# Moving four of a quad's 26 gather operations from the output half to the first-projection half of an expert stage on one Trainium2 core

## The reference

```
g = jax.nn.softmax(cv, axis=-1)
a = jax.nn.gelu(jnp.einsum('td,thkd->thk', tb, u_tab[e]).astype(jnp.float32), approximate=False)
return jnp.einsum('thk,thkd->td', (g * a).astype(tb.dtype), v_tab[e])
```

## Time and profile before

| | |
|---|---|
| median of 3 runs | 4360.06 us (4358.92 to 4373.73) |
| the profiled execution's own time | 4361.63 us |
| its span, first to last instruction | 4359.9 us |
| stage of the experts, within the span | about 2350 to 4280 us |
| busy over the span: PE, DVE, ACT, POOL | 80%, 63%, 31%, 38% |
| DMA over the span | 1001.69 MB, mean 230 GB/s |

### The profile page before, as it was taken

How to read it: one execution, slowest core, us unless ns; L and a number is a source line. 1 busy time by engine, 2 the same in 40 slices (tenths; PEclk the granted TensorE clock), 3 DMA queues, 4 the chain that set the end, 5 groups by cost and what they waited for, 6 DMA issues and landing times. The chain is left out here.

```text
span 4359.9 us, 58885 instructions
## 1 busy us (share of the span) xinstructions
PE 3499.7 (80%) x20213; PEld 2842.0 (65%) x20213; DVE 2764.6 (63%) x5857; ACT 1344.7 (31%) x3219; POOL 1641.3 (38%) x1339
## 2 busy tenths in 40 slices
PE   6899967846577668625665999999999999999995
PEld 1344335521144468625555999999999999999994
DVE  0011148610113403899995998888989989999985
ACT  0111136610001111137783333333333333333331
POOL 0000000000000143238885565565556655556650
PEclk9899979977768889867777999999999999999997
DMA  9345144489931133305547988989889888888984
GB/s 348 133 173 179 60 141 151 133 337 408 406 143 35 50 109 98 96 29 117 129 106 226 324 323 310 323 313 323 319 307 329 322 323 314 318 321 324 322 308 161
DMA packets 390819, 1001.69 MB, mean 230 GB/s; under 512 B 186132, under 2 KB 236143, under 8 KB 327832
## 3 DMA queue, kind: packets, MB, share of 16 engines
q1 hardware_dynamic: 324232, 487.39, 32.7%
q0 software_dynamic: 64144, 474.73, 30.1%
q10 hardware_dynamic: 2272, 37.68, 2.4%
HBM read 914.75 MB, written 152.04 MB: 245 GB/s over the span
## 5 line engine op out<-in xcount | busy, mean ns | idle before, releaser
L1904 DVE CUSTOM_DVE_ANT_0 e_uv<-e_uv,e_h 128x1024 f32<-128x1024 f32 x416 | 720.9, 1733 | 73.4 <-DMA e_uv<-peer_uv,k_g_idx 71.4
L1973 POOL DMA_INDIRECT e_uv<-peer_uv,k_g_idx x416 | 519.5, 1249 | 534.7 <-DVE e_pY L1916 493.5
L1212 PE MATMUL e_pa<-k_hi_d,e_uh 128*128 128x320 f32 x2048 | 639.0, 312 | 65.4 <-POOL e_ul L1964 55.8
L1212 PE MATMUL e_po<-e_ph,e_vh 128*128 128x320 f32 x2048 | 645.0, 315 | 54.3 <-DVE k_OT L1948 49.1
L1214 PE MATMUL e_pa<-k_hi_d,e_ul 128*128 128x320 f32 x2048 | 633.7, 309 | 0.0
L1213 PE MATMUL e_pa<-k_lo_d,e_uh 128*128 128x320 f32 x2048 | 633.7, 309 | 0.0
L1214 PE MATMUL e_po<-e_ph,e_vl 128*128 128x320 f32 x2048 | 632.7, 309 | 0.0
L1213 PE MATMUL e_po<-e_pl,e_vh 128*128 128x320 f32 x2048 | 632.6, 309 | 0.0
L1916 DVE SCALAR_TENSOR_TENSOR e_pY<-e_uv,e_wts,e_pY 128x1024 f32<-128x1024 f32 x412 | 526.1, 1277 | 0.0
L1212 PEld LDWEIGHTS e_pa<-k_hi_d,e_uh 128*128 128x128 f32 x2048 | 385.3, 188 | 77.4 <-issue 64.4
L1212 PEld LDWEIGHTS e_po<-e_ph,e_vh 128*128 128x128 f32 x2048 | 384.3, 188 | 76.6 <-DVE k_OT L1948 63.0
(11 more groups left out here) (280 smaller groups left out, 5460.5 us busy)
## 6 DMA issues: line engine op xcount, KB each, us to landing
s_kv<-kv_pages SPq DMA_DIRECT2D x128, 512.0 KB
s_kv<-kv_state SPq DMA_DIRECT2D x32, 2048.0 KB
e_u<-peer_ut SPq DMA_DIRECT2D x128, 512.0 KB, 6.2
e_v<-peer_uv SPq DMA_DIRECT2D x128, 512.0 KB
s_g<-r_G SPq DMA_DIRECT2D x10, 4096.0 KB, 20.8
k_OT<-s_g SPq DMA_DIRECT2D x128, 320.0 KB
k_win_sample<-state_k_win ACTq DMA_DIRECT2D x28, 1168.0 KB
v_win_sample<-state_v_win POOLq DMA_DIRECT2D x28, 1168.0 KB
```

Of the source, the lines that this page charges most:

```text
L1212: nc.tensor.matmul(out, lhs_hi, rhs_hi, start=start, stop=False)
L1904: nc.vector.tensor_tensor_reduce(uv[:, r, 0:D], uv[:, r, 0:D], h[:], 1.0, 0.0, ALU.mult, ALU.add, dots[:, r:r + 1]).then_inc(row_dotted, 1)
L1973: nc.gpsimd.indirect_dma_start(uv[:, s % RING], None, io["peer_uv"], bass.IndirectOffsetOnAxis(ap=keep.g_idx[:, s:s + 1], axis=0),).then_i ...
```

## The change

`share` deals the same 26 operations, in the same order, over the places in another way. Before, every one of the 16 output places has one, and the eight first-half places have 10 between them (1, 1, 1, 2, 1, 1, 1, 2). Now 12 go to the output places (0, 1, 1, 1 in each group of four) and 14 to the first half (1, 2, 2, 2, 1, 2, 2, 2). Nothing else is edited.

```diff
         def share(slot):
 
+            late = OUTS * 3 // 4
             if slot >= DOTS:
-                first = NR - OUTS + slot - DOTS
-                return range(first, first + 1)
-            return range((NR - OUTS) * slot // DOTS, (NR - OUTS) * (slot + 1) // DOTS)
+                n = slot - DOTS
+                return range(NR - late + n * 3 // 4, NR - late + (n + 1) * 3 // 4)
+            return range((NR - late) * slot // DOTS, (NR - late) * (slot + 1) // DOTS)
```

## The result

The changed kernel takes 4408.55 us (median of 4 runs, 4404.33 to 4411.64), the kernel before 4359.81. The ratio is 1.0103, with a 95% interval of 1.0084 to 1.0121: slower by 1.0%, 49 us, little but clear of the noise. The forecast was 4320, and the range ended at 4390. The profiled execution took 4411.64, with a span of 4409.9.

A forecast was written before the change was run, and what follows sets the result against it. VectorE, late all round the 60.1 us quad, was taken as the bound; orders of 59.5 and 57.2 mixed to 58.7, with transfers 58.8, so 1.3 us x 31 = 40 us gained: 4320 us, range 4272 to 4390.

The forecast's parts named there:

- What bounds the kernel: Whole quad of 60.1 us: VectorE is late all round, and TensorE's 3.8 us of standing still follow from it.
- The arithmetic of the path: Quad period: first add at 33.7, plus 0.45, 21.1 of TensorE output work and 4.2 to the next `e_act`, 59.5 us.
- the point of decision: First half: a first add 34.4 us after the first `e_act`, 60.1 - 25.75, beyond which the change is slower.
- Order A: First half with v of block 3 in time, two subtractions without a gap: first add at 33.7, period 59.5 us.
- Rival (2): First half becomes the long pole, with all 2.2 us of transfer wait moved in: period 61.7, 4411 us; chance 0.20.
- I take 0.8 us, nearer to the low end because of the lead: First-half transfer waits per quad, put at 0.8 us because gathers were thought issued 10 us or more before their dots.
- the upper bound of 2.2: First-half transfer waits: at most the kernel before's gather wait of 2.2 us a quad.
- The last sum: Quad period: 58.7 plus half to all of 0.8 for transfers, taken as 58.8, 59.2 at most; gain 40 us.
- The mixture of orders A and B: Quad period over the stage: 0.65 x 59.5 + 0.35 x 57.2 = 58.7 us, before transfer waits.
- B: First half with v of block 3 some tenths late: 2.4 us of block vanish, first add at 31.3, period 57.2 us.
- from there it runs free: TensorE from output place 4, after the first add at 33.7 + 0.45: 21.1 us without holds to the end of the half.
- The bound by the DMA engines: First half's 11.1 MB at about 358 GB/s from HBM for one core: it could not be shorter than 31.0 us.

The follow-up runs named there:

- e9: Changed kernel with the next gather issued ahead of GpSimd's subtraction of v in first-half place 5 only; 4373.27 us, ratio 1.0056.
- e3: Changed kernel with only the first 512 of 1024 columns of u and v loaded for block c + 2; 4409.06 us, ratio 1.0101.
- e7: Changed kernel with GpSimd's subtraction of v done on 512 of 1024 columns from the second quad on; 4311.29 us, ratio 0.9883.
- e1: Changed kernel with the next gather issued ahead of GpSimd's subtraction of v in first-half places 0 and 5; 4481.16 us, ratio 1.026.
- e5: e1 with 8 overwritten TensorE matmuls added ahead of output place 0 of each quad; 4433.97 us, ratio 1.0167.
- e2: Kernel before the change with the next gather issued ahead of GpSimd's subtraction of v in first-half places 0 and 5; 4470.94 us, ratio 1.0248.

## Why the prediction was wrong

**What bounds the kernel: right.** VectorE was late all round; after the change TensorE is busy in the output half, its waits for adds fell from 49.1 to 21.1 us, and VectorE waits for TensorE at the start of a quad. The arithmetic of the path was right in kind, first half + what TensorE then needs, but that term was taken at 25.75 us and came out at 26.4, so that 35.1 makes 61.5 and not 60.9. With 26.4 the point of decision is a first half of 60.1 - 26.4 = 33.7 us, and not 34.4: in e9 33.9 went with a period of 60.3. Order A, laid out at 33.7, stood on this point and had no gain in it. Rival (2), which was given 0.20, had the direction and gave 4411 for what came out as 4408.6; that closeness is luck, since it rests on 59.5 + 2.2 of transfer waits, and 3.5 were measured with half of the blocks.

**The step that failed: "I take 0.8 us, nearer to the low end because of the lead".** The transfer waits of the first half were 3.5 us a quad, over the upper bound of 2.2 too. The ground for it was that "from the issue of a gather to its dot it is 10 us or more in my layout". That was a misreading of my own layout. The gather that follows a sum belongs to the dot five operations later; seven operations later, at place 4, the layout has the 10 us or more. In the layout the gather of place 0 went out at 4.5 (behind the subtraction) and its dot in place 3 could start at 11.8: 7.3 us, and the quad shown has 7.2, of the 9.7 that it needed. The waits of the kernel before come at leads of the same size, 7.4 us in the mean of its output half, so the lead spoke for the upper end of the bound. Packing the operations shortened just this lead; before, this gather went out at 3025.49, its dot came in place 4, and the lead was 10.4 us in the mean.

**The last sum does not follow either.** From the mixture of 58.7, half to all of the 0.8 is 59.1 to 59.5, not 58.8 and "59.2 at most". By its own terms the prediction had a gain of 0.6 to 1.0 us a quad, 19 to 31 us, and not 40.

**The mixture of orders A and B: wrong.** B rested on v of block 3 coming late, in a third of the quads. It was in time in all of them (the trace after has 0.2 us of such waits in total, the one before 15.6). The likely reason is the gather wait in place 3, which puts everything behind it off; the same shift would explain why the blocks, laid out as 8.0, were 4.1, though no run shows either by itself. The errors cancelled: 8.0 of blocks, 0.8 of gather waits and 2.9 for ScalarE on paper, 4.1, 3.5 and 4.1 in the trace, 11.7 both times. About 1.4 of the last stands in place 1, mostly because TensorE is late there. The first half came out at 35.1 instead of 33.7 to 34.5; the 0.6 above the upper end are small gaps, for which the layout had nothing.

**Order A itself was priced too low.** Its first half was near (34.1 in e3), but "from there it runs free" was not right: the hold for `e_pl` of place 6, which comes at 28.3 when TensorE is through with its half at 24.4, was in the layout, and I priced it as nothing but a hold. In most quads of e3 the granted clock falls behind it. The quads of e3 in which this hold stands take 61.6 us with the fall and 60.1 without, not 59.5. So even the case on which the forecast stood was at or above the 60.1 of the kernel before.

**The bound by the DMA engines** was not the cause: e3 with 2.1 MB less a quad took the same time as the change. The Trainium skill's page DMA: Bandwidth & Descriptors was used for a floor of 31.0 us of the first half. The page gives its 358 GB/s (Specifications) as half of what two cores share, and says further down (Measured) that it is about what each gets when both stream. As a limit of this core it does not hold: the trace before moved 407 GB/s in the mean from 981 to 1199 us (the row below), nearly all of it loads of `kv_pages` and `kv_state` into SBUF. The mean first half with 14 operations and all of the traffic was 32.0 us at the least (e7), so that nothing was run below 31.0. "Nearly what the engines have moved here at best" was true of the 25 us slices of this stage only:

```profile
DMA packets 15991, 88.72 MB, mean 407 GB/s; under 512 B 2022, under 2 KB 2022, under 8 KB 13417
```

What stays open is how the loss divides between blocks and held gathers in the changed kernel itself. They trade against each other from run to run (3.5 and 4.1 in the change, 0.5 and 8.1 in e1, 1.1 and 5.6 in e3), and only the shorter subtraction lowered both by much. A fifth ring buffer, which would lengthen every lead without moving an instruction, was not tried.

## What to carry to other kernels

When operations are moved from one stretch to another, what they meet there counts more than their own time: lay out the other engines' instructions beside them, and follow every transfer from its issue to the instruction that uses it, by name. Balance in sums (43.2 us of VectorE's work beside 56.3 of TensorE's) says little where one engine blocks another by the instruction; here 4.7 us of moved work made a half 6.8 us longer. And a hold of TensorE can have a price beyond its length: look at the spacing of the matmuls behind it before a hold is called free.

## What the runs showed of the hardware

- TensorE stood still for 2.2 to 2.6 us in most quads of the change, e1 and e3, and in 19, 24 and 21 of 30 quads the matmuls behind such a hold stood 0.27 us apart instead of 0.147, at a granted clock of 0.51 to 0.53, the lower level (1.2 GHz). It does not follow every time: in the change 17 of the 30 holds at place 6 had it. In e5, where eight filler matmuls left 1.3 us of the hold, one quad of 30 had a fall, at another place, and the kernel was 47 us faster than e1. In e3 quads with the same hold and the same first half took 1.5 us longer with the fall than without it.
- VectorE's instructions with two SBUF inputs stood still behind GpSimd's subtractions, and through two or four of them that followed without a gap (3.38 and 4.71 us). The Trainium skill's page SBUF — State Buffer says that the loser of the shared port pair fully blocks for the whole instruction; these rows agree (2.74 instead of 1.21 us), and add that the block did not end with the instruction where GpSimd had the next one ready. GpSimd waited in its turn: a subtraction took 3.45 us instead of 2.41 when VectorE's dot had begun just before it.
- Moving one gather issue by one instruction on GpSimd, in two places of each quad, cost 73 us (e1) and 109 us (e2).
